# MLP up tiles as 512-column matmuls over high and low rows, with the rows' two parts stored next to each other

## The chip, the cores and the metric

The kernel runs on one core of one Trainium2 chip. The metric is the device time of one execution in microseconds. Before the change it is 1320.01 us, the median of 3 runs (1319.76 to 1320.15).

## The reference

One sequence of 256 tokens with 1024 features goes through two stacks in float32. The first stack: an RMS norm and an input projection; two recurrent mixers (a gated delta rule and HGRN2) on halves of the features; an output projection; the MLP; a gated embedding. The second stack: a convolution mixer with 16 meta tokens ahead of the sequence, then a product-key expert layer over 16384 experts, computed densely, and a final norm. The part that the change is about is the MLP of the first stack:

```python
u = jnp.einsum('btd,df->btf', rms_norm(h, pre_mlp_norm[i]), w_mlp_up[i])
y = jnp.einsum('btf,fd->btd', jnp.square(jax.nn.relu(u)), w_mlp_down[i])
h = h + rms_norm(y, post_mlp_norm[i])
```

with `w_mlp_up` of 1024 x 4096 and `w_mlp_down` of 4096 x 1024.

## The kernel before

**Weights.** All large weights are one stream of tiles of 128 x 1024 float32 values (512 KB), which SyncE loads into a ring of four slots. Each tile is split into two float32r parts: ScalarE copies the high part `w_hi` (`hi`, L1285 to L1292), and VectorE, or GpSimd in some stages, subtracts it from the tile to get the low part `w_lo` (`lo`, L1898 to L1904). There are two slots for the parts (`S = 2`), so the split of tile g+2 waits until TensorE has used tile g. The rows x, kept transposed in `hT_hi` and `hT_lo`, are split in the same way. A product is three matmuls: high by high, the weights' high by the rows' low, the weights' low by the rows' high.

**Rows.** `hT_hi` and `hT_lo` are two tensors of 8 blocks of 128 features; a block has META + T = 272 columns (16 meta tokens, 256 tokens), 1088 bytes in each partition. Six times in the kernel the normalised rows are transposed into them: for the input projection, the output projection, the MLP, the gate, the second input projection, and the query projection with the experts' first layer. `hT_at` (L344) tells where the 256 tokens begin: column 0 or, for the gate and the second input projection, column 16.

**Two kinds of tile.** `out_block` (L618) makes features by tokens: the stationary operand is a 128 x 128 block of the weights, the moving operand 256 columns of the rows. `passes` (L600) puts out the matmuls: for each of 8 blocks k the pair `w_hi` by high rows and `w_hi` by low rows, then the signal `hi_used`, a wait for `lo_done`, and 8 matmuls with `w_lo`; 24 in all, in one bank's first 256 columns. `row_tile` (L653) makes tokens by features: the stationary operand is 128 tokens of the rows, the moving operand 512 columns of the weights; 12 matmuls. `first_block` (L623) is the first tile after a transposition and mixes the three kinds of product, since its rows come block by block. Tiles of the first kind are the f, q and qkv projections (20 tiles), the MLP's up tiles (32), the second input projection (20), the query projection (16) and the experts' first layer (128). Tiles of the second kind are the i, z and g projections (12, through `rows_of`), the output projections, the MLP's down tiles (32), the embedding, the gate and the experts' second layer.

**The MLP.** It has four rounds of 8 up tiles and 8 down tiles. An up tile m writes bank 4 + m % 4. When it is done, ScalarE takes Relu of the bank into `relu` (L1479), and VectorE squares it into `mid` (L2187), casts that to `mid_hi` (L2190) and subtracts to get `mid_lo` (L2192). Each step waits for the one before by a semaphore (`relu_out`, `mid_step`, `mid_out`). The down tiles accumulate into banks 0 to 3, with `mid_hi` and `mid_lo` as stationary operands. The order on each engine is the order in which the code lists it: on ScalarE the split of a later tile's `w_hi` and then Relu, on VectorE the split of `w_lo` and then the three steps.

## Time and profile before

| | us |
|---|---|
| median of 3 runs | 1320.01 |
| the profiled execution | 1318.27 |
| its span, from the first to the last instruction | 1316.5 |
| TensorE busy with matmuls | 1291.7 |
| VectorE busy | 1007.4 |
| ScalarE busy | 789.9 |
| GpSimd busy | 444.6 |

The time of an execution is longer than its span by what lies around the first and the last instruction. Times are microseconds, from the span's start, unless marked ns. PE is TensorE's matmul side, DVE is VectorE, ACT is ScalarE. A tile's name stands for the tensor (`arena` is the big buffer that holds `relu`, `mid` and much else; `bank` is one of 8 PSUM banks). In the view of groups a line has the code line, the engine, the operation, output<-inputs, shapes, the count, and after the bar the busy time, the mean duration of one, and the idle time ahead of it with what ended it. The durations of matmuls are from the start to the modelled end, and neighbours overlap. In the timeline a line begins with the start and the duration; a number after x says how many instructions were merged.

### The profile page before, as it was taken

The page shows a single profiled execution, that of the slowest core. Times are in us where ns is not written, and L with a number is a line of the kernel's source. Part 1 is how long each engine was busy: PE and PEld are TensorE (multiplying, and loading weights), DVE is VectorE, ACT ScalarE, POOL GpSimd, SP SyncE. Part 2 cuts the span into 40 slices and gives each one's busy share as a digit, 9 for nine tenths or more (in the row PEclk, how much of TensorE's full clock was granted, in tenths as well). Part 3 has the DMA queues.
Part 4 walks back from the last instruction along what each step waited for, and adds up shares of the span by engine and source line. Part 5 has one row for each costly group of instructions (what it writes and reads, how often), then busy time and mean ns, then how long its engine had stood idle before and what let it go on. Part 6 is the DMA issues. An engine that isn't in the chain of part 4 may idle for free.

```text
span 1316.5 us, 24954 instructions
## 1 busy us (share of the span) xinstructions
PE 1291.7 (98%) x8852; PEld 1183.3 (90%) x8852; DVE 1007.4 (77%) x1890; ACT 789.9 (60%) x1414; POOL 444.6 (34%) x255
## 2 busy tenths in 40 slices
PE   7999999999999999999999999999999999999997
PEld 7998988989977997999999999999998888888886
DVE  4787658656666985689997777887636899999996
ACT  6545445444466455467776777777656566666664
POOL 2100415000023754038888777777750000000000
PEclk9999999999999999999999999999999999999999
DMA  8533126666654544555656555555567666555553
GB/s 304 177 113 113 33 96 203 191 191 191 184 169 134 170 132 130 171 161 177 190 179 188 161 161 161 160 161 160 158 195 224 222 197 206 199 201 192 195 190 112
DMA packets 64657, 225.49 MB, mean 171 GB/s; under 512 B 7200, under 2 KB 7712, under 8 KB 64176
## 3 DMA queue, kind: packets, MB, share of 16 engines
q1 hardware_dynamic: 62832, 218.36, 53.1%
q10 hardware_dynamic: 1728, 5.84, 1.2%
q8 instruction: 61, 1.00, 0.3%
q14 instruction: 36, 0.29, 0.1%
HBM read 223.12 MB, written 1.05 MB: 170 GB/s over the span
## 4 chain that ended last, share of the span: by engine, by line
PE 93%; DVE 4%; issue 1%; ACT 1%; DMA 0%; POOL 0%; SPq 0%; POOLq 0%; DVEq 0%; ACTq 0%
PE bank L613 76%; PE bank L1154 2%; PE bank L1185 2%; PE bank L1182 2%; PE bank L1181 2%; PE bank L714 1%; PE bank L862 1%; PE bank L848 1%; DVE w_lo L1903 1%; PE bank L1109 1%; PE bank L595 1%; PE bank L670 0%; DVE arena L2269 0%; PE bank L1017 0%; DMA cols<-in_cols 0%
## 5 line engine op out<-in xcount | busy, mean ns | idle before, releaser
L1292 ACT ACTIVATE w_hi<-ring 128x1024 fp32r<-128x1024 f32 x380 | 402.5, 1060 | 381.4 <-issue 197.5
L613 PE MATMUL bank<-hT_hi,w_hi 128*128 128x256 f32 (+2 forms) x1696 | 420.3, 286 | 0.0
L613 PE MATMUL bank<-hT_lo,w_hi 128*128 128x256 f32 (+2 forms) x1696 | 412.6, 282 | 0.0
L1903 DVE TENSOR_TENSOR w_lo<-ring,w_hi 128x1024 fp32r<-128x1024 f32 x225 | 275.3, 1224 | 143.1 <-ACT w_hi L1292 140.1
L1855 POOL TENSOR_TENSOR w_lo<-ring,w_hi 128x1024 fp32r<-128x1024 f32 x128 | 310.9, 2431 | 143.0 <-ACT w_hi L1292 142.8
L613 PEld LDWEIGHTS bank<-hT_lo,w_hi 128*128 128x128 f32 x1696 | 320.0, 189 | 0.4
L613 PEld LDWEIGHTS bank<-hT_hi,w_hi 128*128 128x128 f32 x1696 | 318.9, 188 | 0.4
L613 PE MATMUL bank<-hT_hi,w_lo 128*128 128x256 f32 (+2 forms) x1696 | 234.8, 280 | 0.0
L613 PEld LDWEIGHTS bank<-hT_hi,w_lo 128*128 128x128 f32 x1696 | 215.9, 189 | 0.0
L1752 POOL TENSOR_SCALAR mstat<-mstat 128x1 f32<-128x1 f32 x16 | 6.1, 383 | 537.7 <-ACT bank L1249 334.4
L613 PE MATMUL bank<-w_hi,wgt_hi 128*128 128x512 f32 x368 | 143.4, 390 | 0.2 <-DVE wgt_lo L2515 0.2
L613 PE MATMUL bank<-w_hi,wgt_lo 128*128 128x512 f32 x368 | 143.2, 389 | 0.0
L613 PE MATMUL bank<-w_lo,wgt_hi 128*128 128x512 f32 x368 | 98.4, 389 | 0.0
L1646 ACT ACTIVATE wgt_hi<-arena 128x256 fp32r<-128x256 f32 x116 | 47.0, 406 | 63.6 <-PE bank L613 60.5
L613 PEld LDWEIGHTS bank<-w_hi,wgt_hi 128*128 128x128 f32 x368 | 69.1, 188 | 15.3 <-issue 1.1
L613 PEld LDWEIGHTS bank<-w_lo,wgt_hi 128*128 128x128 f32 x368 | 69.1, 188 | 14.4
L613 PEld LDWEIGHTS bank<-w_hi,wgt_lo 128*128 128x128 f32 x368 | 69.1, 188 | 14.2
L1634 ACT ACTIVATE consts<-consts,idxT 128x128 f16<-128x128 f16 x256 | 81.1, 392 | 0.0
L1816 POOL TENSOR_TENSOR w_lo<-ring,w_hi 128x1024 fp32r<-128x1024 f32 x26 | 62.8, 2414 | 25.9 <-ACT w_hi L1292 24.5
L2515 DVE TENSOR_TENSOR wgt_lo<-arena,wgt_hi 128x256 fp32r<-128x256 f32 x128 | 55.3, 432 | 5.4 <-ACT wgt_hi L1646 5.4
L2502 DVE TENSOR_TENSOR arena<-arena,bank 128x256 f32<-128x256 f32 (+35 forms) x80 | 24.4, 305 | 41.9 <-ACT bank L1620 19.0
L2480 DVE TENSOR_TENSOR consts<-bank,idxT 128x512 f16<-128x512 f32 x64 | 44.2, 691 | 12.1 <-ACT consts L1634 9.8
(395 smaller groups left out, 2077.8 us busy)
## 6 DMA issues: line engine op xcount, KB each, us to landing
ring<-in_stream SPq DMA_DIRECT2D x380, 512.0 KB, 3.6
arena<-in_stream SPq DMA_DIRECT2D x34, 512.0 KB, 4.6
arena<-in_rows ACTq DMA_DIRECT2D x1, 1536.0 KB, 10.8
consts<-in_consts ACTq DMA_DIRECT2D x1, 1152.0 KB, 6.0
arena<-in_keys ACTq DMA_DIRECT2D x1, 1024.0 KB, 5.0
h<-in_x SPq DMA_DIRECT2D x2, 256.0 KB, 3.9
h<-in_x ACTq DMA_DIRECT2D x2, 256.0 KB, 3.9
arena<-in_rows ACTq DMA_DIRECT2D x1, 512.0 KB, 4.6
```

Of the source, the lines that this page charges most:

```text
L613: mm = nc.tensor.matmul(o, a, b, start=first and not low_part and xp is x[0], stop=last and low_part)
L1154: mm = nc.tensor.matmul(bank[half][:, n * P:(n + 1) * P], hot2[:, half, n, :], hotg[:, half, i, n, :], start=i == 0, stop=i == 1)
L1181: nc.tensor.matmul(bank[b][:, :], x[0], w, start=first and b >= 4, stop=False)
L1182: nc.tensor.matmul(bank[b][:, :], x[1], w, start=False, stop=False)
L1292: nc.scalar.activation(w_hi[:, g % S, :], ring[:, g % R, :], ACT.Copy).then_inc(hi_done, 1)
L1634: ins = nc.scalar.activation(hotg[:, s % 2, 0, n, :], hot1[:, n, :], ACT.Copy, scale=idxT[:, 2, 4 * s + n:4 * s + n + 1])
L1646: nc.scalar.activation(wgt_hi[:, j % 2, :], act_all[:, at, :], ACT.Copy).then_inc(wgt_step, 1)
L1816: nc.gpsimd.tensor_tensor(w_lo[:, g % S, :], ring[:, g % R, :], w_hi[:, g % S, :].bitcast(F32), ALU.subtract).then_inc(lo_done, 1)
L1855: nc.gpsimd.tensor_tensor(w_lo[:, g % S, :], ring[:, g % R, :], w_hi[:, g % S, :].bitcast(F32), ALU.subtract).then_inc(lo_done, 1)
L1903: nc.vector.tensor_tensor(w_lo[:, g % S, :], ring[:, g % R, :], w_hi[:, g % S, :].bitcast(F32), ALU.subtract).then_inc(lo_done, 1)
L2480: nc.vector.tensor_tensor(hot1, over(iota_bank, 4), spread(idxT[:, 0, tok], P), ALU.is_equal)\
L2515: nc.vector.tensor_tensor(wgt_lo[:, j % 2, :], at, wgt_hi[:, j % 2, :].bitcast(F32), ALU.subtract)\
```

## The change

It does four things.

1. The two tensors become one, `hT`, and a second view of the same bytes is added: `x_both`, with 8 blocks of 2048 bytes in each partition, 256 high columns and then 256 low ones. The four stages without meta tokens use this view (`x_hi`, `x_lo`, `x_cut`); the gate and the second input projection keep the old one.
2. An up tile of the MLP (`up_block`) issues for each block k one matmul of 512 columns, `w_hi` by high and low rows together, and then the 8 matmuls of `w_lo` by the high rows as before. High products and low products of the rows thus stand in the two halves of a bank. The first up tile writes its low products to the second half too, with the old 24 matmuls.
3. The sum of the halves and the activation: ScalarE copies the low half to `up`, VectorE adds the other half from the bank, and then makes max(u, 0) * u in one instruction.
4. The cast to `mid_hi` moves from VectorE to ScalarE, and it and the subtraction for `mid_lo` come one tile later in their engines' order, behind the split of the next weights.

```diff
@@ -147,8 +147,10 @@
         ring = sb("ring", [P, R, D])
         w_hi = sb("w_hi", [P, S, D], F32R)
         w_lo = sb("w_lo", [P, S, D], F32R)
-        hT_hi = sb("hT_hi", [P, KD, META + T], F32R)
-        hT_lo = sb("hT_lo", [P, KD, META + T], F32R)
+        hT = sb("hT", [P, 2, KD, META + T], F32R)
+        hT_hi, hT_lo = hT[:, 0, :, :], hT[:, 1, :, :]
+        x_both = hT.rearrange("p a k n -> p (a k n)")[:, 0:2 * KD * T].rearrange("p (k a t) -> p k a t", k=KD, a=2)
+        x_hi, x_lo = x_both[:, :, 0, :], x_both[:, :, 1, :]
         h = sb("h", [P, NT, D])
         consts = sb("consts", [P, NCONST])
         cols = sb("cols", [P, NCOLS])
...
@@ -341,7 +343,8 @@
                 eng.wait_ge(tiles_done, rows_end[stage])
 
         block_cols = ["pre_mix", None, "pre_mlp", None, "mix2", "ffn2"]
-        hT_at = [0, 0, 0, META, META, 0]
+        rows_in_view = [(x_hi, x_lo) if n not in (3, 4) else (hT_hi[:, :, META:META + T], hT_lo[:, :, META:META + T])
+                        for n in range(6)]
 
         def block_scale(n, k):
 
...
@@ -492,6 +495,8 @@
         yT_high, yT_ready = sem("yT_high"), sem("yT_ready")
         keys_loaded, scores_full = sem("keys_loaded"), sem("scores_full")
 
+        up_low, up_low0 = vt_out, 1
+        mid_high, mid_high0 = kt_out, 1
         pair_loaded, pair_loaded0 = meta_in_sb, 16
         pair_sums, pair_sums0 = dbias, 2
         pair_hi, pair_hi0 = decays, 2
...
@@ -615,14 +623,29 @@
                 mm.then_inc(tiles_done, 1)
                 return mm
 
-            def out_block(w, o, cols_of):
-
-                passes(w, [(o, hT_cut(k, cols_of), slice(k * P, (k + 1) * P), True, k == 0, k == KD - 1)
+            def out_block(w, o, rows_of=x_cut):
+
+                passes(w, [(o, rows_of(k), slice(k * P, (k + 1) * P), True, k == 0, k == KD - 1)
                            for k in range(KD)])
 
-            def first_block(w, o, cols_of, n, lag=0):
+            def up_block(w, b):
 
                 slot, low = w
+                both = bank[b][:, :]
+                for k in range(KD):
+                    mm = nc.tensor.matmul(both, w_hi[:, slot, k * P:(k + 1) * P], x_both[:, k, :, :],
+                                          start=k == 0, stop=False)
+                mm.then_inc(hi_used, 1)
+                pe.wait_ge(lo_done, low)
+                for k in range(KD):
+                    mm = nc.tensor.matmul(bank[b][:, 0:T], w_lo[:, slot, k * P:(k + 1) * P], x_hi[:, k, :],
+                                          start=False, stop=k == KD - 1)
+                mm.then_inc(tiles_done, 1)
+
+            def first_block(w, o, n, lag=0, rows_of=x_cut, apart=None):
+
+                slot, low = w
+                o_low = o if apart is None else apart
 
                 def part(k):
                     return slice(k * P, (k + 1) * P)
...
@@ -631,20 +654,20 @@
 
                     if k == 0:
                         pe.wait_ge(lo_done, low)
-                    return nc.tensor.matmul(o, w_lo[:, slot, part(k)], hT_hi[:, k, cols_of], start=False, stop=k == KD - 1)
+                    return nc.tensor.matmul(o, w_lo[:, slot, part(k)], rows_of(k)[0], start=False, stop=k == KD - 1)
 
                 if tr_bank[n]:
                     pe.wait_ge(tr_lo, KD * n + 2)
                 for k in range(KD):
                     pe.wait_ge(tr_hi, KD * n + k + 1)
-                    nc.tensor.matmul(o, w_hi[:, slot, part(k)], hT_hi[:, k, cols_of], start=k == 0, stop=False)
+                    nc.tensor.matmul(o, w_hi[:, slot, part(k)], rows_of(k)[0], start=k == 0, stop=False)
                     if lag <= k < KD - 1 + lag:
                         low_product(k - lag)
                     if k:
                         pe.wait_ge(tr_lo, KD * n + k)
-                        nc.tensor.matmul(o, w_hi[:, slot, part(k - 1)], hT_lo[:, k - 1, cols_of], start=False, stop=False)
+                        nc.tensor.matmul(o_low, w_hi[:, slot, part(k - 1)], rows_of(k - 1)[1], start=False, stop=False)
                 pe.wait_ge(tr_lo, KD * n + KD)
-                nc.tensor.matmul(o, w_hi[:, slot, part(KD - 1)], hT_lo[:, KD - 1, cols_of], start=False, stop=False)\
+                nc.tensor.matmul(o_low, w_hi[:, slot, part(KD - 1)], rows_of(KD - 1)[1], start=False, stop=False)\
                     .then_inc(hi_used, 1)
                 for k in range(KD - max(lag, 1), KD):
                     mm = low_product(k)
...
@@ -925,7 +948,7 @@
                     mm.then_inc(oa_full, 1)
 
             def out_lhs(j, t):
-                return hT_cut(OUT_ORDER[j], slice(t * P, (t + 1) * P))
+                return x_cut(OUT_ORDER[j], slice(t * P, (t + 1) * P))
 
             pe.wait_ge(gdn_gated, 4)
             for j in range(6):
...
@@ -955,8 +978,8 @@
                 s = (G_MLP + m) % S
                 pe.wait_ge(hi_done, i * 16 + (G_MLP + m + 1))
 
-                pe.wait_ge(relu_out, i * 8 + m + 1)
-                out_block((s, i * 16 + (G_MLP + m + 1)), bank[4 + m % 4][:, 0:T], slice(0, T))
+                pe.wait_ge(up_out, i * 8 + m + 1)
+                up_block((s, i * 16 + (G_MLP + m + 1)), 4 + m % 4)
 
             def mlp_round(i, closing):
 
...
@@ -1279,7 +1302,7 @@
                     if k % 2 == 0:
                         act.wait_ge(tr_full, 4 * n + k // 2 + 1)
                     src = bank[tr_bank[n] + k // 2][:, (k % 2) * T:(k % 2 + 1) * T]
-                    nc.scalar.activation(hT_hi[:, k, hT_at[n]:hT_at[n] + T], src, ACT.Copy, scale=block_scale(n, k))\
+                    nc.scalar.activation(rows_in_view[n][0][:, k, :], src, ACT.Copy, scale=block_scale(n, k))\
                         .then_inc(tr_hi, 1)
 
             def hi(g, round_=0, per=0):
...
@@ -1471,14 +1493,21 @@
 
             def mlp_round(i, closing):
 
+                def mid_copy(m):
+
+                    act.wait_ge(mid_step, i * 8 + m + 1)
+                    nc.scalar.activation(mid_hi[:, m, :], mid[:, m % 2, :], ACT.Copy).then_inc(mid_high, 1)
+
                 for m in range(8):
                     hi(G_MLP + m + S, i, 16)
+                    if m:
+                        mid_copy(m - 1)
                     act.wait_ge(tiles_done, i * 16 + (G_MLP + m + 1))
-
-                    act.wait_ge(mid_out, i * 8 + m + 1)
-                    nc.scalar.activation(relu[:, m % 2, :], bank[4 + m % 4][:, 0:T], ACT.Relu).then_inc(relu_out, 1)
+                    nc.scalar.activation(up[:, m % 2, :], bank[4 + m % 4][:, T:2 * T], ACT.Copy).then_inc(up_low, 1)
                 for m in range(8, 14 if closing else 16):
                     hi(G_MLP + m + S, i, 16)
+                    if m == 8:
+                        mid_copy(7)
                     if closing and m < 12:
                         h_squares(2, 0, m - 8)
 
...
@@ -2177,22 +2206,31 @@
             dve.wait_ge(lo_done, G_MLP + 1)
             los(G_OUT + 7, 1)
             dve.sem_inc(mid_out, 2)
+            dve.sem_inc(up_out, 4)
+
+            def mid_low(i, m):
+
+                dve.wait_ge(mid_high, i * 8 + (mid_high0 + m + 1))
+                nc.vector.tensor_tensor(mid_lo[:, m, :], mid[:, m % 2, :], mid_hi[:, m, :].bitcast(F32),
+                                        ALU.subtract).then_inc(mid_out, 1)
 
             def mlp_round(i, closing):
 
                 for m in range(8):
                     lo(G_MLP + m + S, i, 16)
-
-                    dve.wait_ge(relu_out, i * 8 + m + 5)
-                    nc.vector.tensor_tensor(mid[:, m % 2, :], relu[:, m % 2, :], relu[:, m % 2, :], ALU.mult)\
-                        .then_inc(mid_step, 1)
-                    dve.wait_ge(mid_step, i * 16 + 2 * m + 1)
-                    nc.vector.tensor_copy(mid_hi[:, m, :], mid[:, m % 2, :]).then_inc(mid_step, 1)
-                    dve.wait_ge(mid_step, i * 16 + 2 * m + 2)
-                    nc.vector.tensor_tensor(mid_lo[:, m, :], mid[:, m % 2, :], mid_hi[:, m, :].bitcast(F32),
-                                            ALU.subtract).then_inc(mid_out, 1)
+                    if m:
+                        mid_low(i, m - 1)
+
+                    dve.wait_ge(up_low, i * 8 + (up_low0 + m + 1))
+                    nc.vector.tensor_tensor(up[:, m % 2, :], up[:, m % 2, :], bank[4 + m % 4][:, 0:T], ALU.add)\
+                        .then_inc(up_out, 1)
+                    dve.wait_ge(up_out, i * 8 + m + 5)
+                    nc.vector.scalar_tensor_tensor(mid[:, m % 2, :], up[:, m % 2, :], 0.0, up[:, m % 2, :],
+                                                   ALU.max, ALU.mult).then_inc(mid_step, 1)
                 for m in range(8, 14 if closing else 16):
                     lo(G_MLP + m + S, i, 16)
+                    if m == 8:
+                        mid_low(i, 7)
 
             with dve.Fori(0, MLP_ROUNDS - 1) as i:
                 mlp_round(i, False)
```

The query projection and the experts' tiles change in the same way as the projections, `hT_cut(k, slice(0, T))` to `x_cut(k)`.

## Rows read from the trace of the kernel before

**Rows 1.** The page's busy times, and the chain that ended last by engine.

```profile
PE 1291.7 (98%) x8852; PEld 1183.3 (90%) x8852; DVE 1007.4 (77%) x1890; ACT 789.9 (60%) x1414; POOL 444.6 (34%) x255
...
PE 93%; DVE 4%; issue 1%; ACT 1%; DMA 0%; POOL 0%; SPq 0%; POOLq 0%; DVEq 0%; ACTq 0%
```

**Rows 2.** Windows, MLP: length, busy of PE, PEld, DVE, ACT, POOL, clock, DMA.

```profile
201.00:380.00 179.00, 178.86 (x1154) 162.86 (x1152) 116.47 (x171) 83.78 (x115) 21.26 (x31) 1.00 0.63 190
```

**Rows 3.** Groups by form, whole span: a 256-column product, two 256-wide operations.

```profile
L613 PE MATMUL bank<-hT_hi,w_hi 128*128 128x256 f32 x1576 | 389.1, 285 | 0.0
...
L1646 ACT ACTIVATE wgt_hi<-arena 128x256 fp32r<-128x256 f32 x116 | 47.0, 406 | 63.6 <-PE bank L613 60.5 <-PE bank L1185 3.1
...
L2269 DVE SCALAR_TENSOR_TENSOR arena<-bank,cols,arena 128x256 f32<-128x256 f32 x104 | 43.0, 476 | 2.9 <-ACT arena L1533 2.5
```

**Rows 4.** Timeline of TensorE, up tiles: starts of three, one's w_lo products.

```profile
254.77 0.28 PE L613 MATMUL bank<-hT_hi,w_hi 128*128 128x256 f32 x1
...
256.67 1.11 PE L613 MATMUL bank<-hT_hi,w_lo 128*128 128x256 f32 x8
257.61 0.28 PE L613 MATMUL bank<-hT_hi,w_hi 128*128 128x256 f32 x1
...
260.45 0.28 PE L613 MATMUL bank<-hT_hi,w_hi 128*128 128x256 f32 x1
```

**Rows 5.** Timeline of TensorE, down tiles: the first matmul of two neighbours.

```profile
235.37 0.39 PE L613 MATMUL bank<-w_hi,mid_hi 128*128 128x512 f32 x1
...
238.09 0.39 PE L613 MATMUL bank<-w_hi,mid_hi 128*128 128x512 f32 x1
```

**Rows 6.** Timeline of TensorE, output projection: first matmuls for k = 7, 0, 1.

```profile
182.55 0.40 PE L613 MATMUL bank<-w_hi,hT_hi 128*128 128x512 f32 x1
...
185.35 0.39 PE L613 MATMUL bank<-w_hi,hT_hi 128*128 128x512 f32 x1
...
188.09 0.40 PE L613 MATMUL bank<-w_hi,hT_hi 128*128 128x512 f32 x1
```

**Rows 7.** Chain in order of time (start, us, what): two tiles of the projections.

```profile
109.43 2.84 PE bank L613 x12
...
114.21 2.79 PE bank L613 x12
```

**Rows 8.** Timeline of TensorE, products with wab_both: blocks 0, 1, 4, 5; what follows.

```profile
53.34 0.28 PE L736 MATMUL bank<-hT_hi,wab_both 128*16 128x256 f32 x1
...
53.57 0.28 PE L736 MATMUL bank<-hT_hi,wab_both 128*16 128x256 f32 x1
...
54.27 0.28 PE L736 MATMUL bank<-hT_hi,wab_both 128*16 128x256 f32 x1
...
54.50 0.28 PE L736 MATMUL bank<-hT_hi,wab_both 128*16 128x256 f32 x1
...
55.19 0.28 PE L613 MATMUL bank<-hT_hi,w_hi 128*128 128x256 f32 x1
```

**Rows 9.** Timeline of VectorE, one up tile and the next split.

```profile
249.53 1.23 DVE L1903 TENSOR_TENSOR w_lo<-ring,w_hi 128x1024 fp32r<-128x1024 f32 x1 [1.67 <-ACT w_hi L1292]
250.67 0.42 DVE L2187 TENSOR_TENSOR arena<-arena 128x256 f32<-128x256 f32 x1
251.12 0.29 DVE L2190 CAST mid_hi<-arena 128x256 fp32r<-128x256 f32 x1
251.45 0.43 DVE L2192 TENSOR_TENSOR mid_lo<-arena,mid_hi 128x256 fp32r<-128x256 f32 x1
252.37 1.23 DVE L1903 TENSOR_TENSOR w_lo<-ring,w_hi 128x1024 fp32r<-128x1024 f32 x1 [0.49 <-ACT w_hi L1292]
```

**Rows 10.** Timeline of ScalarE, one up tile.

```profile
256.87 1.06 ACT L1292 ACTIVATE w_hi<-ring 128x1024 fp32r<-128x1024 f32 x1 [1.43 <-PE bank L613]
257.89 0.38 ACT L1479 ACTIVATE arena<-bank 128x256 f32<-128x256 f32 x1
```

**Rows 11.** Windows, columns as before: a stretch of the query projection.

```profile
521.00:524.00 3.00, 3.00 (x15) 3.00 (x15) 3.00 (x7) 1.12 (x4) 0.00 (x0) 0.50 0.53 175
```

45 lines of the change are left out of this document (23 added, 22 removed).

## The prediction

> **What bounds the kernel now.** I read the page's busy times first, and then the chain that ended last: TensorE is busy for 98% of the span and holds 93% of the chain [rows 1]. Next comes the stretch of the MLP, 201 to 380 us: TensorE is busy for 178.86 of the 179.00 us at the full clock, VectorE for 116 and ScalarE for 84 [rows 2]. So in the MLP a nanosecond counts only if TensorE saves it, and the other engines matter only once they make it wait. The view of groups says how one matmul looks, but its mean (285 ns) is from start to end of instructions that overlap [rows 3]. What a matmul costs is the distance between starts, so I go to the timeline. An up tile is 24 matmuls of 256 columns; three tiles start at 254.77, 257.61 and 260.45, so a tile takes 2.84 us and a matmul 118.3 ns [rows 4]. A down tile is 12 matmuls of 512 columns and takes 2.72 us, 226.7 ns each [rows 5]. Both send 6144 columns, which at 2.4 GHz is 2.56 us. What is above that is a surcharge per matmul: 0.28 us over 24 is 11.7 ns, 0.16 us over 12 is 13.3 ns. It hardly depends on the width, so fewer and wider matmuls are cheaper.
>
> **The change, part by part.**
>
> *The up tiles on TensorE.* In a tile, 16 matmuls of 256 columns (w_hi against high and low rows) become 8 of 512; the 8 of w_lo stay at 256. The before trace has no 512-column matmul with x as the moving operand, but the down tiles have the same form, with a stationary 128x128 block and 512 moving columns that begin on a multiple of 2048 bytes. I take their price: 8 x 226.7 + 8 x 118.3 = 2760 ns against 2840, so 80 ns a tile [rows 4, 5]. 31 of the 32 up tiles take the new form; the first one (`first_block`) keeps its 24 matmuls and only puts the low products in the other half of the bank. 31 x 0.080 = **2.5 us less**, all of it on the path, since the engine is never idle there [rows 2]. Bounds: 0, if two 256-column matmuls with one block cost no more than one of 512; and 31 x 8 x 13.3 ns = 3.3 us, if every removed matmul takes the larger surcharge with it.
>
> A sentence by itself: the Trainium skill, page "TensorE: Matmul & The Clock Gate", section "Back-to-back issue gap", puts the warm gap at N/2.4 + 2.5 ns; by it two matmuls of 256 columns cost 218.3 ns and one of 512 215.8, which would make this term 31 x 8 x 2.5 ns = 0.6 us. The trace does not agree: its two widths carry 11.7 and 13.3 ns [rows 4, 5].
>
> *The layout as stationary operand.* In the i, z and g projections (12 tiles) and the output projection (8 tiles) the rows are the stationary operand. Before, a block k begins at 1088 x k bytes, afterwards every piece begins on a multiple of 512. The timeline has both cases: the output tile that starts at 182.55 (k = 7, off a multiple of 256) takes 2.80 us, the next one (k = 0, on it) 2.74 [rows 6], and the down tiles, always on one, 2.72 [rows 5]. The pieces of the chain in the projections take 2.79 to 2.84 us for their 12 matmuls [rows 7]. I take 0.07 x 12 = 0.84 us there and 0.08 for the 6 output tiles other than k = 0 and 4, 0.48 us: **1.3 us less**. Bounds: 0 (it isn't the address), and 20 tiles x 0.10 = 2.0 us. The gate tiles keep the old view with its 16 columns ahead, and change nothing.
>
> *The layout as moving operand.* This is the uncertain part, because it reaches far beyond the MLP. The group of 256 columns has 1576 of each of its three kinds of product, 197 tiles [rows 3]. Without the 4 tiles that stay in the old view, and counting what is left of the up tiles and three first tiles, that is 162 x 24 + 31 x 8 + 3 x 24 = 4208 matmuls whose moving rows now begin on a multiple of 1024 bytes. In no tile before do all the moving blocks lie on such addresses. The nearest row is that of the 16 small products with `wab_both`: from 53.34 to 55.19, 115.6 ns each, with moving rows on every residue of the old layout and a stationary block of only 16 columns [rows 8]. Lower bound: 115.6, so 4208 x -2.7 = -11.4 us. Upper bound: the surcharge of the 512-column matmuls, whose operands are all aligned, 106.7 + 13.3 = 120.0 ns, so 4208 x 1.67 = +7.0 us. I take **0**: the up tiles keep 2.84 us exactly although their eight blocks lie on eight different residues [rows 4], which speaks for a rate that the address doesn't set. Both ends go into the range.
>
> *VectorE in an up tile.* Before: w_lo split, square, cast, subtraction; starts at 249.53, 250.67, 251.12, 251.45, end at 251.88, and the next split at 252.37 after 0.49 us of idle time [rows 9]. After: w_lo split (1.14 to the next start), `mid_low` of the tile before (0.45), the addition that reads the bank (0.48 at most, as the operation that reads a bank in [rows 3], plus 0.05 for its semaphore), max-times (0.43): 2.55 us in a period of 2.76. Cost 0; TensorE hides it. 0.2 us of slack is left of 0.49.
>
> *ScalarE.* Before: w_hi split 1.06 and Relu 0.38 [rows 10]. After: 1.06 + the copy to `mid_hi` (0.41, [rows 3]) + the copy of the low half (0.38) = 1.85 us of 2.76. There is a new wait: `mid_copy(m-1)` waits for VectorE's max-times of m-1. Queued behind it on ScalarE are the copy of tile m, for which VectorE's addition waits, and the w_hi split of tile m+3. In time after the end of tile m: ScalarE's split ends at about +0.3 (it starts 0.2 after the w_lo products begin [rows 4, 10]), the copies end at +0.7 and +1.1. VectorE is through its split at +1.5 and `mid_low` at +1.9, adds until +2.4 and has the product at +2.85. The copy that needs it wants to start at 2.76 + 0.3 = +3.06. It fits with 0.2 us. TensorE needs w_hi of m+2 at +2.76, has it at +0.3; and the bank of tile m four tiles later. Cost 0. If the cover went, the loop ScalarE-VectorE would set the tile time, and 0.1 us too much is 31 x 0.1 = 3.1 us.
>
> *The rest.* The first down tile of a round wants `mid_low(0)`, which was made six tiles earlier; `mid_low(7)` is made during the first down tiles and used by the eighth. SP's ring loads keep their order and gates; a tile period of 2.76 us asks for less than the 2.72 of the down tiles gets now. The pair products address the same bytes as before. All 0, and could not gain.
>
> **Sum.** -2.5 - 1.3 + 0 = -3.8 us. The profiled execution took 1318.27 us (span 1316.5 and 1.8 around it): 1314.5. It lies 1.74 below the median of the runs, 1320.01, so for the median: **1316.2 us**.
>
> **The rivals.**
> *A, aligned 256-column matmuls are slower.* The end on the other side. Mechanism: if the surcharge belongs to the addresses as in the all-aligned down tiles, each of the 4208 costs up to 120.0 ns. For: 13.3 is more than 11.7 [rows 4, 5]. Against: the wider matmul also moves twice the data, and among the `wab_both` products the block at residue 0 is no slower than that at residue 256 (0.23 us for either pair) [rows 8]. Price up to +7.0: 1323.2. It cancels the gain from 0.9 ns per matmul (119.2) and makes the kernel slower by over 0.2% from 1.5 ns.
> *B, they are faster.* For: alignment helps the stationary operand by 6 ns [rows 6], so it may help the moving one. Against: the constant 2.84. Half of the lower bound, 117.0 ns, gives -5.7: 1310.5; all of it 1304.8.
> *C, the ScalarE-VectorE loop becomes the bound* in the up tiles, with a new wait in place of covered work. For: slack falls from 0.49 to 0.2. Against: the sum above. At 0.1 us a tile: 1319.3.
> *D, the change doesn't do what it says:* 8 x 512 take as long as 16 x 256, since the block's load was hidden anyway. Only the stationary part remains: 1318.7. Against: [rows 4, 5].
> *E, the clock.* Three stretches ran at half clock, 1.2 GHz, one of them at 521 to 524 us, in the first tile of the query projection [rows 11]; 15 of its matmuls took 3.00 us instead of 1.78, some 1.4 us over the whole stretch. All work behind the MLP comes 3 us earlier, so one such stretch may go or come: 1314.8 or 1317.6.
>
> **How the numbers follow.** Forecast 0.50 (its own range 1314.2 to 1318.2, 0.4 ns per aligned matmul and E's small shifts), A 0.18, B 0.18, C 0.05, D 0.05, E alone 0.04. 0.2% is 2.6 us, about what can be told from no change: faster means below 1317.4. Faster: 0.36 of the forecast's 0.50, 0.17 of B, 0.01 of E = 0.54. Same: 0.14 + 0.08 of A + 0.01 of B + 0.03 of C + 0.05 of D + 0.02 of E = 0.33. Slower: 0.10 of A + 0.02 of C + 0.01 of E = 0.13. The range leaves out the far half of B (0.09) and the far end of A (0.04) and little else: 1310.0 to 1322.5.
>
> **What would show it.** Up tiles that start 2.76 us apart, 226.7 ns between 512-column matmuls and 118.3 between the w_lo ones; output tiles at 2.72; tiles of the query projection and of the expert stage still at 2.84 (2.86 and above is A, 2.81 and below B, and there the whole forecast stands or falls); idle time of some 0.2 us before VectorE's split, and none on TensorE between 204 and 372 us. It is wrong if the expert tiles change, if the up tiles stay at 2.84, or if TensorE waits in them for the bank or for `w_hi`.

## The result, and the profile after the change

The changed kernel takes 1321.99 us (median of 12 runs, 1320.26 to 1324.15) against 1319.84 for the kernel before in the same runs (12 runs, 1316.92 to 1321.62): ratio 1.0021, interval 1.0013 to 1.0029. It is slower by 0.2%, where 1316.2 was forecast. The profiled execution took 1320.26 us, its span 1318.4.

The page's busy times and the chain by engine, which answer to [rows 1]:

```profile
PE 1292.8 (98%) x8604; PEld 1174.5 (89%) x8604; DVE 1006.1 (76%) x1890; ACT 798.3 (61%) x1446; POOL 443.9 (34%) x255
...
PE 93%; DVE 4%; issue 1%; ACT 1%; POOL 0%; ACTq 0%; POOLq 0%; DVEq 0%
```

248 matmuls are gone (8852 to 8604), and yet TensorE is busy for 1.1 us more. Nothing else moved on the chain. So the loss is in how long matmuls take, and I add up stages. Each goes from its first start on TensorE to the first start of what follows; the MLP and the experts' second layer go to the start of their last matmul.

| stage | before | after | difference | forecast |
|---|---|---|---|---|
| input projections up to the i tiles (with wab) | 64.94 | 65.64 | +0.70 | 0 |
| i, z, g tiles and what follows them | 93.24 | 92.85 | -0.39 | -0.84 |
| output projection | 27.13 | 26.77 | -0.36 | -0.48 |
| MLP | 178.05 | 176.51 | -1.54 | -2.5 |
| query projection and the experts' first layer | 451.87 | 455.81 | +3.94 | 0 |
| experts' second layer | 337.72 | 337.45 | -0.27 | 0 |

The differences add up to +2.1 us, as the two executions and the medians differ (+2.0, +2.15).

The timeline of TensorE in the changed kernel's MLP, columns as in [rows 4] (start, duration, instruction, how many merged):

```profile
254.14 2.00 PE L636 MATMUL bank<-hT,w_hi 128*128 128x512 f32 x8
255.98 1.12 PE L641 MATMUL bank<-hT,w_lo 128*128 128x256 f32 x8
256.94 2.00 PE L636 MATMUL bank<-hT,w_hi 128*128 128x512 f32 x8
258.78 1.11 PE L641 MATMUL bank<-hT,w_lo 128*128 128x256 f32 x8
```

An up tile takes 256.94 - 254.14 = 2.80 us (2.793 on average) where [rows 4] had 2.84 and 2.76 was forecast. The eight wide matmuls last 1.84 us to the start of the `w_lo` products, 230 ns each instead of 226.7.

The windows that answer to [rows 2] and [rows 11], columns as there:

```profile
201.00:378.00 177.00, 176.85 (x906) 151.05 (x904) 116.99 (x170) 91.47 (x147) 20.56 (x31) 1.00 0.63 192
```

```profile
521.00:524.00 3.00, 2.99 (x24) 2.80 (x24) 2.51 (x4) 1.33 (x2) 0.00 (x0) 1.00 0.29 117
```

TensorE waits no more than before, 0.15 us in 177. The stretch at half clock of [rows 11] is not there: the granted clock is 1.00 in it. That gave something back, so the loss in the experts is larger than 3.94; against `wide_only` below (451.00 us, full clock there too) it is 4.81.

Where it comes from shows in two w_lo groups of neighbouring expert tiles, first of the kernel before, then of the changed one:

```profile
641.77 1.11 PE L613 MATMUL bank<-hT_hi,w_lo 128*128 128x256 f32 x8
...
644.61 1.11 PE L613 MATMUL bank<-hT_hi,w_lo 128*128 128x256 f32 x8
```

```profile
640.66 1.12 PE L621 MATMUL bank<-hT,w_lo 128*128 128x256 f32 x8
...
643.54 1.12 PE L621 MATMUL bank<-hT,w_lo 128*128 128x256 f32 x8
```

2.84 us apart, then 2.88: 118.3 ns a matmul before and 120.0 after, with the same instructions in the same order. In the view of groups 2656 high and 1328 low products of this form are left outside the up tiles:

```profile
L621 PE MATMUL bank<-hT,w_hi 128*128 128x256 f32 x2656 | 351.6, 285 | 0.0
L621 PE MATMUL bank<-hT,w_lo 128*128 128x256 f32 x1328 | 186.1, 283 | 0.0
```

The high products' mean is the 285 ns of [rows 3], so the loss is easily overlooked in this view. It measures overlapping instructions from start to end, and its means also mix stages: inside the experts' loop alone the mean goes from 281 to 283 ns.

The output projection, which answers to [rows 6]:

```profile
182.70 1.98 PE L621 MATMUL bank<-w_hi,hT 128*128 128x512 f32 x8
...
185.42 1.98 PE L621 MATMUL bank<-w_hi,hT 128*128 128x512 f32 x8
...
188.14 1.07 PE L621 MATMUL bank<-w_hi,hT 128*128 128x512 f32 x4
```

Both tiles take 2.72 us, as forecast for rows as the stationary operand on multiples of 512.

VectorE and ScalarE in an up tile, which answer to [rows 9] and [rows 10]:

```profile
257.28 1.23 DVE L1932 TENSOR_TENSOR w_lo<-ring,w_hi 128x1024 fp32r<-128x1024 f32 x1 [0.44 <-ACT w_hi L1315]
258.42 0.42 DVE L2214 TENSOR_TENSOR mid_lo<-arena,mid_hi 128x256 fp32r<-128x256 f32 x1
258.76 0.41 DVE L2225 TENSOR_TENSOR arena<-arena,bank 128x256 f32<-128x256 f32 x1
259.20 0.42 DVE L2228 SCALAR_TENSOR_TENSOR arena<-arena 128x256 f32<-128x256 f32 x1
260.07 1.23 DVE L1932 TENSOR_TENSOR w_lo<-ring,w_hi 128x1024 fp32r<-128x1024 f32 x1 [0.44 <-ACT w_hi L1315]
```

```profile
256.18 1.06 ACT L1315 ACTIVATE w_hi<-ring 128x1024 fp32r<-128x1024 f32 x1 [1.16 <-PE bank L636]
257.15 0.40 ACT L1499 ACTIVATE mid_hi<-arena 128x256 fp32r<-128x256 f32 x1
257.45 0.37 ACT L1506 ACTIVATE arena<-bank 128x256 f32<-128x256 f32 x1
```

VectorE still has 0.44 us of idle time in a period of 2.79 (0.2 was forecast), and ScalarE 1.16. Their new work costs nothing.

### The profile page after: what moved, and what is told of

Same layout as the page of the kernel before. It is cut to its first block, busy times and chain, and to the rows that moved or that the text cites. A ratio compares the mean times of both kernels' runs of the same rounds, so it can differ in the third digit from the quotient of the medians.

```text
span 1318.4 us, 24443 instructions
## 1 busy us (share of the span) xinstructions
PE 1292.8 (98%) x8604; PEld 1174.5 (89%) x8604; DVE 1006.1 (76%) x1890; ACT 798.3 (61%) x1446; POOL 443.9 (34%) x255
## 4 chain that ended last, share of the span: by engine, by line
PE 93%; DVE 4%; issue 1%; ACT 1%; POOL 0%; ACTq 0%; POOLq 0%; DVEq 0%
PE bank L621 69%; PE bank L636 4%; PE bank L1177 2%; PE bank L641 2%; PE bank L1204 2%; PE bank L1205 2%; PE bank L1208 2%; PE bank L737 1%; PE bank L885 1%; DVE w_lo L1932 1%; PE bank L871 1%; PE bank L1132 1%; PE bank L693 0%; DVE arena L2307 0%; PE bank L1040 0%
## 5 line engine op out<-in xcount | busy, mean ns | idle before, releaser
L621 PE MATMUL bank<-hT,w_hi 128*128 128x256 f32 (+1 forms) x2896 | 384.7, 285 | 0.0
L621 PEld LDWEIGHTS bank<-hT,w_hi 128*128 128x128 f32 x2896 | 360.1, 191 | 0.6
L621 PE MATMUL bank<-hT,w_lo 128*128 128x256 f32 (+1 forms) x1448 | 203.2, 283 | 0.0
L621 PEld LDWEIGHTS bank<-hT,w_lo 128*128 128x128 f32 x1448 | 187.0, 192 | 0.0
L636 PE MATMUL bank<-hT,w_hi 128*128 128x512 f32 x248 | 62.0, 392 | 0.0
L636 PEld LDWEIGHTS bank<-hT,w_hi 128*128 128x128 f32 x248 | 44.8, 189 | 8.1
```

The source lines that it names most:

```text
L621: mm = nc.tensor.matmul(o, a, b, start=first and not low_part and xp is x[0], stop=last and low_part)
L636: mm = nc.tensor.matmul(both, w_hi[:, slot, k * P:(k + 1) * P], x_both[:, k, :, :], start=k == 0, stop=False)
```

## The experiments

The question is what makes the unchanged 256-column matmuls slower, and what the wide ones are worth without it. In the experiments the places of the rows are a table, `X_AT`: for stage 0 (input projections), 1 (output projection), 2 (MLP) and 5 (query projection and experts) the column where the high rows begin, the column where the low ones begin, and the distance between blocks, in columns of 4 bytes. A stage that is not in it keeps the old places. The code fixes distances, not addresses: `w_hi`, `w_lo` and `hT` stand one behind the other, `w_hi` and `w_lo` take 8192 bytes each, and weight blocks are 512 bytes apart, so offset 0 is a multiple of 512 bytes away from every weight block. Where the first tensor begins is up to the build, and no run here varies it. So "on a multiple of 512" in the texts below, and "residue", are to be read as a distance from the weights. Of each edit only the table is shown; the code that reads it is left out, and lines that begin with `+#` are explanations. Columns of the fences are those of [rows 4].

### One part alone: layout_only and wide_only

`layout_only` is the kernel before with the new places and the 24 narrow matmuls:

```diff
+X_AT = {0: (0, 256, 512), 1: (0, 256, 512), 2: (0, 256, 512), 5: (0, 256, 512)}
```

> The kernel before with nothing changed but the place of the rows: blocks of 2048 bytes, high next to low, in the four stages without meta tokens. Up tiles keep their 24 matmuls of 256 columns. Address theory (a 256-column matmul whose operands all begin on multiples of 512 bytes carries the surcharge of the down tiles, 13.3 ns, 120.0 in all): up tiles and expert tiles 2.88 us instead of 2.84, 195 tiles and three first ones, so 198 x 0.04 = +7.9 us, less 1.3 us for the rows as stationary operand: +6.6 us, 1326.4. Rival, the new ScalarE-VectorE chain or the 512-column matmuls cost the time: expert tiles stay at 2.84, and the kernel is 1.3 us faster than before.

`wide_only` is the changed kernel with the new places in the MLP alone:

```diff
-        x_both = hT.rearrange("p a k n -> p (a k n)")[:, 0:2 * KD * T].rearrange("p (k a t) -> p k a t", k=KD, a=2)
...
+        X_AT = {2: (0, 256, 512)}
```

> The changed kernel with the new places for the rows in the MLP alone; the input, output and query projections and the experts have the old blocks of 1088 bytes. Address theory: the expert tiles are back at 2.84 us, the MLP keeps the 1.5 us that it gained in the changed kernel (up tiles 2.79), so 1.5 us faster than before, 1318.3. Rival, the expert stage is slower for another reason (its first tile, the clock, the order in front of it): it stays at 455.8 us from the first query tile to the first second-layer tile, and the kernel is slower than before by some 2 us.

Both against 1318.88 us for the kernel before: `layout_only` 1324.94 (ratio 1.0042, 1.0027 to 1.0056), `wide_only` 1316.51 (0.9979, 0.9970 to 0.9989). Expert tiles of `layout_only`, then of `wide_only`:

```profile
640.07 1.12 PE L632 MATMUL bank<-hT,w_lo 128*128 128x256 f32 x8
...
642.95 1.12 PE L632 MATMUL bank<-hT,w_lo 128*128 128x256 f32 x8
```

```profile
641.57 1.10 PE L637 MATMUL bank<-hT,w_lo 128*128 128x256 f32 x8
...
644.41 1.10 PE L637 MATMUL bank<-hT,w_lo 128*128 128x256 f32 x8
```

2.88 us with the new places and 2.84 without them; the query projection and the experts take 455.82 us in `layout_only`, as in the changed kernel (455.81). So the places make the loss there, all of it, and the MLP goes from 178.05 to 176.46 us in `wide_only`. Of its 2.4 us, 0.87 are in the query projection and the experts (451.00 for 451.87), where the half-clock stretch at 521 us is missing too.

The places cost something in the MLP as well: with narrow matmuls at the new places (`layout_only`) it takes 179.21 us, with wide ones at the same places 176.51. At equal places the wide form saves 2.70 us, 87 ns a tile, and 40 ns of these only make good what the places cost. The two halves of the change pull against each other, and the layout, which serves the MLP's 31 tiles, is charged to 144 others and to the 20 of the first projections.

### Which property of the places: residues_a and residues_b

Three things changed at once: the residue of the start, the high rows' block lying next to the low one, and that all blocks have the same residue. Each stage tries another combination.

```diff
+# residues_a: 64 bytes later; blocks of 2112 bytes in the MLP; high and low apart, on multiples of 512, in the experts
+X_AT = {0: (16, 272, 512), 1: (0, 256, 512), 2: (0, 256, 528), 5: (0, 2176, 256)}
+# residues_b: high and low apart; output 2112; MLP blocks of 2176 bytes; experts 64 bytes later
+X_AT = {0: (0, 2176, 256), 1: (0, 256, 528), 2: (0, 256, 544), 5: (16, 272, 512)}
```

> The kernel before, with another place of the rows in each stage, to read the time of a 256-column matmul in the trace. First projections: blocks of 2048 bytes, all 64 bytes past a multiple of 512. MLP: blocks of 2112 bytes, so that the eight blocks lie on eight residues of 512 as before, with high next to low. Query and experts: high blocks of 1024 bytes on multiples of 512, the low ones 8704 bytes on. Three theories. T1, a block on a multiple of 512 is slow in itself: 118 or less in the projections, 118.3 in the MLP, 120.0 in the experts. T2, high next to low is slow: 120.0, 120.0, 118.3. T3, an equal place of all blocks is slow and changing residues are fast: 120.0, 118.3, 120.0.

> As the run before, with the places exchanged. First projections: high blocks of 1024 bytes on multiples of 512, low ones 8704 bytes on. Output projection: blocks of 2112 bytes. MLP: blocks of 2176 bytes, residues 0, 128, 256, 384. Query and experts: blocks of 2048 bytes, all 64 bytes past a multiple of 512. T1 (multiples of 512 are slow): 120.0, MLP between 118.3 and 120.0, experts 118 or less. T2 (neighbours are slow): 118.3, 120.0, 120.0. T3 (equal places are slow): 120.0, 118.3, 120.0.

Times of one run each: 1322.59 and 1315.12. The input projections of `residues_a` (64 bytes later), then those of `residues_b` (apart, on multiples of 512):

```profile
34.37 1.07 PE L632 MATMUL bank<-hT,w_lo 128*128 128x256 f32 x8
...
37.09 1.07 PE L632 MATMUL bank<-hT,w_lo 128*128 128x256 f32 x8
```

```profile
34.59 1.12 PE L632 MATMUL bank<-hT,w_lo 128*128 128x256 f32 x8
...
37.47 1.12 PE L632 MATMUL bank<-hT,w_lo 128*128 128x256 f32 x8
```

2.72 against 2.88 us. Blocks of the same size and neighbourhood as in the changed kernel, only 64 bytes later, cost 113.3 ns a matmul and not 120.0 in the first seven tiles, and 117.8 in some of the later ones. High and low far apart changes nothing. In the MLP, blocks that run over all residues (2112 bytes) give 2.84 as in [rows 4], and blocks on 0 and 128 modulo 256 give 2.81. So it is the residue (T1), and neither the neighbourhood nor the equal places.

A tile is not the mean of its residues, though. T1 had 2.84 to 2.88 for the mix of 0 and 128, and 2.81 is less than a tile with all blocks on 0 (2.88) or all on 128 (2.85, below). What the trace of the kernel before shows is that the starts within an up tile are 115 to 122 ns apart, in the same pattern in every tile. The 2.84 that looked constant was a sum over unequal distances; how a matmul's neighbours enter into them stays open.

### Which residues: uniform_a, uniform_b, wide_a, wide_b

```diff
+# uniform_a, narrow: 128 bytes in the projections, 256 in the MLP, 192 in the experts
+X_AT = {0: (32, 288, 512), 1: (0, 256, 512), 2: (64, 320, 512), 5: (48, 304, 512)}
+# uniform_b, narrow: 32, 128 (output), 384 (MLP), 448 (experts)
+X_AT = {0: (8, 264, 512), 1: (32, 288, 512), 2: (96, 352, 512), 5: (112, 368, 512)}
+# wide_a, 512-column up tiles: 16, 256 (output), 64 (MLP), blocks of 2176 bytes (experts)
+X_AT = {0: (4, 260, 512), 1: (64, 320, 512), 2: (16, 272, 512), 5: (0, 256, 544)}
+# wide_b, 512-column up tiles: 320, 0, blocks of 2112 bytes (MLP), 256 (experts)
+X_AT = {0: (80, 336, 512), 1: (0, 256, 512), 2: (0, 256, 528), 5: (64, 320, 512)}
```

> The kernel before with blocks of 2048 bytes, high next to low, all eight at one distance past a multiple of 512: 128 bytes in the first projections, 256 in the MLP, 192 in the query projection and the experts; the output projection on multiples of 512. What is known: at distance 0 a 256-column matmul takes 120.0 ns, at 64 it took 117.8 in the experts and either 113.3 or 117.8 in the projections. Theory X (only a start on a multiple of 512 is slow): 118 or less at 128, 256 and 192, so tiles of 2.83 us or less. Rival Y (what counts is whether the start is a multiple of 256, as for the rows as stationary operand): 120.0 at 256, so MLP up tiles of 2.88; 118 or less at 128 and 192. Rival Z (a multiple of 128 is slow): 120.0 at 128 and 256.

> As the run before, with distances of 32 bytes in the first projections, 384 in the MLP, 448 in the query projection and the experts, and 128 in the output projection. X: 118 ns or less everywhere. Y: the same. Z: 120.0 at 384, 118 or less at 32 and 448. The output projection (rows as stationary operand, 512 columns) is expected at 2.79 to 2.80 us a tile, since 128 is not a multiple of 256. If the rate has two states at one distance, as at 64 bytes, tiles of 2.72 and of 2.83 us stand side by side in one stage.

> The changed kernel (512-column matmuls in the up tiles) with other distances past a multiple of 512: 16 bytes in the first projections, 256 in the output projection, 64 in the MLP, and blocks of 2176 bytes (distances 0, 128, 256, 384) for the query projection and the experts. If the 27 ns by which the eight 512-column matmuls of an up tile exceed 8 x 226.7 come from starts on a multiple of 512, the up tile falls from 2.79 to 2.74 us or less; if they come from the change of width after the 256-column matmuls, it stays at 2.79 (w_lo products at 117.8 would take 17 ns off). Experts: 117.2 ns as the MLP had with this place, 2.81 us a tile, so 3 us less than before in the stage. Output projection at 2.72 us a tile (256 is as good as 0).

> The changed kernel with distances of 320 bytes in the first projections, 0 in the output projection, blocks of 2112 bytes in the MLP (eight distances) and 256 bytes for the query projection and the experts. X: 118 ns or less at 256, experts 2.83 us. Y and Z: 120.0, 2.88. The up tile with eight distances: 2.79 us or more, if unequal places hinder the 512-column matmul as they do the 256-column one (118.3 against 117.8), 2.74 if they don't.

One run each, beside 1318.34 for the kernel before: 1309.59, 1310.18, 1314.26, 1320.90. First the MLP of `uniform_a` at 256 bytes, then its query projection at 192:

```profile
252.34 1.12 PE L632 MATMUL bank<-hT,w_lo 128*128 128x256 f32 x8
...
255.22 1.12 PE L632 MATMUL bank<-hT,w_lo 128*128 128x256 f32 x8
```

```profile
570.14 1.07 PE L632 MATMUL bank<-hT,w_lo 128*128 128x256 f32 x8
571.05 1.98 PE L632 MATMUL bank<-hT,w_hi 128*128 128x256 f32 x16
572.87 1.07 PE L632 MATMUL bank<-hT,w_lo 128*128 128x256 f32 x8
```

2.88 and 2.73. A start 256 bytes later is as slow as 0, so X (only multiples of 512 are slow) is refuted and Y fits there. At 128 and 384 Y's "118 or less" is missed by a little, and most tiles at 384 take Z's 120.0. The output projection of `uniform_b` takes 2.79, as expected. Over all runs the narrow tiles, 24 matmuls each, are these:

| start of the moving rows, bytes | us a tile | ns a matmul |
|---|---|---|
| 0 or 256 | 2.880 | 120.0 |
| 128 | 2.847 | 118.6 |
| 384 | 2.845 to 2.852 for seven tiles, then 2.880 | 118.5 to 120.0 |
| 16 | 2.847, 2.80 and, for two tiles, 2.72 | 118.6, 116.7, 113.3 |
| 32 | 2.80 | 116.7 |
| 64, 192, 320, 448 | 2.827 or 2.720 | 117.8 or 113.3 |
| over all residues (before) | 2.840 | 118.3 |
| 0 and 128 by turns | 2.813 | 117.2 |

The odd multiples of 64 have two rates, and groups of 8 short matmuls between tiles switch between them. In the query projection of `uniform_a` the rate changes at every such group, from 2.720 to 2.828 and back; the experts' loop, which has none, runs at 2.827 throughout, and from the point where the gate groups (8 short matmuls behind a tile) begin, tiles take 2.720, or 2.813 to 2.818 with the step after the group in it. Stage 5 took 441.10 us at 192 and 440.32 at 448, against 451.87 before; before and at 192 it holds a stretch of 3.4 us at half clock, at 448 none.

The four odd multiples are not alike there. In all runs with 192 or 448 the gate stretch is fast. With 64 (`residues_b`, 449.54 us) it stays at 2.827, and the query projection too.

In the up tiles the wide form reacts in another way. The MLP of `wide_a`, 64 bytes later:

```profile
251.89 2.00 PE L652 MATMUL bank<-hT,w_hi 128*128 128x512 f32 x8
253.72 1.07 PE L657 MATMUL bank<-hT,w_lo 128*128 128x256 f32 x8
254.63 1.99 PE L652 MATMUL bank<-hT,w_hi 128*128 128x512 f32 x8
256.46 1.11 PE L657 MATMUL bank<-hT,w_lo 128*128 128x256 f32 x8
```

Here tiles mostly alternate between 2.741 and 2.772 us, on average the 2.76 of the forecast: the eight wide matmuls last 1.83, where they last 1.84 in the changed kernel, and the narrow ones 0.91 or 0.94 instead of 0.95. At residues of 2112-byte blocks (`wide_b`) an up tile takes 2.80. So for the wide ones 64 bytes make next to nothing, and the aligned place costs the tile through its `w_lo` products. Neither reading of the up tiles in the expectation came out: of the 27 ns above 8 x 226.7, 16 remained. Its output tiles (2.72) and its expert tiles (2.81) did.

### The changed kernel 64 bytes later: shift_64

```diff
-        x_both = hT.rearrange("p a k n -> p (a k n)")[:, 0:2 * KD * T].rearrange("p (k a t) -> p k a t", k=KD, a=2)
+        x_both = hT.rearrange("p a k n -> p (a k n)")[:, 16:16 + 2 * KD * T].rearrange("p (k a t) -> p k a t", k=KD, a=2)
```

> The changed kernel with one number changed: the view of the rows begins 64 bytes later, so that no block begins on a multiple of 256. If the place of the moving rows is what made the changed kernel slower than before, the expert tiles fall from 2.88 us to 2.83 in the first 48 and to 2.72 or 2.81 after the first gate group, as they did in the runs at distances 192 and 448: the stage takes 441 us instead of 455.8. The first projections take 63.8 instead of 65.6, the MLP 175.7 instead of 176.5, and the projections with the rows as stationary operand lose 0.9: some 16 us less than the changed kernel, 1306. Rival (distance 64 is worse than 192 and 448 in the experts, as its steady 2.83 in the loop showed before the gate groups; the other two had the same there): 453 us for the stage, 1318.

1314.63 us against 1318.84, ratio 0.9961 (0.9946 to 0.9975). One number in the changed kernel turns it from 0.2% slower to 0.4% faster. The expectation was too good by 8 us, because I had counted on the rate of 113.3 in the experts. The expert tiles stayed at 2.83 instead:

```profile
639.97 1.10 PE L621 MATMUL bank<-hT,w_lo 128*128 128x256 f32 x8
640.91 2.05 PE L621 MATMUL bank<-hT,w_hi 128*128 128x256 f32 x16
642.79 1.10 PE L621 MATMUL bank<-hT,w_lo 128*128 128x256 f32 x8
```

Behind the loop, after six short matmuls, two tiles fell to 2.72 (from 705.57 to 708.29; in `residues_b` they didn't), and the first gate group threw them back to 2.827, with 2.913 to 2.918 for the tiles behind a gate group (`uniform_a`: 2.813 to 2.818). The stage took 449.22, near the 449.54 of `residues_b`, also at 64: the rival, that 64 is worse than 192 and 448 in the experts, is what came, if not in its full size (453). As the stationary operand, 64 bytes cost: the output projection takes 27.30 us, 0.5 more than in the changed kernel. The i, z and g stage takes 94.37, but it begins with a stretch at reduced clock that lasted longer here (granted 0.67 from 76 to 86 us, 0.83 in the changed kernel); against `layout_only`, which had 0.70 there and 94.12 us, 0.25 more is left.

### The best of each: best and best_kick

```diff
+# 64 bytes for projections and MLP, 0 for the output projection, 192 for query and experts
+X_AT = {0: (16, 272, 512), 1: (0, 256, 512), 2: (16, 272, 512), 5: (48, 304, 512)}
```

> The changed kernel with a place of the rows for each stage: 64 bytes past a multiple of 512 in the first projections and the MLP, on multiples of 512 in the output projection (stationary operand), 192 bytes past in the query projection and the experts. By the sums of the stages measured one by one: first projections -1.2 us against the kernel before, output projection -0.4, MLP -2.4, query and experts -10.8: 15 us less, 1304.

`best_kick` adds eight matmuls with zeros behind expert tile 1 (counted from 0), to push the loop from one rate to the other. For that, the first four expert tiles are written out ahead of the loop:

```diff
+            for e in range(PEER_BODY):
+                w = tile(G_PEER + e)
+                pe.wait_ge(gel_out, e + 1)
+                out_block(w, bank[4 + e][:, 0:T])
+                if e == 1:
+                    pe.wait_ge(sc_out, NHH // 2)
+                    for n in range(8):
+                        nc.tensor.matmul(bank[0][:, 0:P], zb, zb, start=True, stop=True)
```

> The run before with 8 small matmuls of zeros (bf16, 128 columns) after the second expert tile, into a bank that is free then, and the first four expert tiles written out instead of looped. The 256-column matmuls at odd multiples of 64 bytes have run at 113.3 or at 117.8 ns in one and the same stage, and changed from the slower to the faster state at the first gate group. If the group's small matmuls are what changed it, the 44 tiles of the loop now take 2.72 us instead of 2.83: 0.107 x 44 = 4.7 us less than the run before, less 0.5 us for the small matmuls: 1300. If it was something else (the end of the loop, the transposes of the routing), no change or 0.5 us more.

`best`: 1304.21 us against 1318.84, ratio 0.9884 (0.9868 to 0.9901). `best_kick`: 1302.61, ratio 0.9880 (0.9863 to 0.9896). The experts' loop in `best`, then in `best_kick`, from its tile 1 on:

```profile
640.87 1.11 PE L637 MATMUL bank<-hT,w_lo 128*128 128x256 f32 x8
641.81 2.05 PE L637 MATMUL bank<-hT,w_hi 128*128 128x256 f32 x16
643.70 1.11 PE L637 MATMUL bank<-hT,w_lo 128*128 128x256 f32 x8
```

```profile
575.52 1.10 PE L637 MATMUL bank<-hT,w_lo 128*128 128x256 f32 x8
576.47 0.62 PE L1173 MATMUL bank<-zeros 128*128 128x128 bf16 x8
576.90 2.07 PE L637 MATMUL bank<-hT,w_hi 128*128 128x256 f32 x16
578.80 1.07 PE L637 MATMUL bank<-hT,w_lo 128*128 128x256 f32 x8
...
641.93 1.07 PE L637 MATMUL bank<-hT,w_lo 128*128 128x256 f32 x8
...
644.65 1.07 PE L637 MATMUL bank<-hT,w_lo 128*128 128x256 f32 x8
```

2.827 against 2.720: the same instructions at the same places, and eight short matmuls some tiles ahead decide which. The rate changes at the zeros: the two written-out tiles ahead of them still run at the slow rate, the next one starts its matmuls 113 ns apart. So writing the tiles out is not what does it.

Stage 5 falls from 441.10 to 437.41 us, but 0.8 of these 3.7 us is the clock: the first query tile takes 5.01 us in `best` (granted clock 0.66) and 4.23 in `best_kick` (1.00). The rest, 2.9 us, is what the other rate is worth, where 4.2 were expected: three tiles took 3.0 us, TensorE waiting 0.2 us in each for GpSimd's split of `w_lo`, and the last of the loop 3.08. The medians differ by 1.6 us where their intervals overlap, so that the second is faster than the first as a whole isn't shown; that its loop runs at the other rate is.

### Address or distance: weights_off

The weights stayed where they were until here, so the residue of the rows could be one of their address or of their distance from the weights. This kernel moves `w_hi` and `w_lo` by 64 bytes, with the narrow up tiles.

```diff
+        sb("ahead_of_weights", [P, 16])
         w_hi = sb("w_hi", [P, S, D], F32R)
         w_lo = sb("w_lo", [P, S, D], F32R)
+        sb("behind_weights", [P, 112])
+X_AT = {0: (16, 272, 512), 1: (0, 256, 512), 2: (0, 256, 512), 5: (48, 304, 512)}
```

> The kernel before (24 matmuls of 256 columns in the up tiles) with all weight parts w_hi and w_lo moved 64 bytes past a multiple of 512, and rows at 64 in the first projections, at 0 in the output projection and the MLP, at 192 in the query projection and the experts. If what counts is the distance between moving and stationary address (R), the rates move with it: 120.0 ns in the first projections (difference 0), and the MLP's up tiles fast, 2.83 us or less (difference 64). If each address counts by itself (S), the MLP stays at 120.0 or gets slower still, since its stationary operand now starts off a multiple of 256 (+6 ns for the 512-column matmuls), and the down tiles, whose moving operand now starts at 64, tell what that does to 512 columns: 2.72 us if nothing.

1321.35 us (one run). Its input projections, rows and weights both 64 bytes off, and its MLP, rows at 0 and weights at 64:

```profile
34.94 1.12 PE L634 MATMUL bank<-hT,w_lo 128*128 128x256 f32 x8
35.90 2.08 PE L634 MATMUL bank<-hT,w_hi 128*128 128x256 f32 x16
37.82 1.12 PE L634 MATMUL bank<-hT,w_lo 128*128 128x256 f32 x8
```

```profile
250.41 1.07 PE L634 MATMUL bank<-hT,w_lo 128*128 128x256 f32 x8
251.32 1.98 PE L634 MATMUL bank<-hT,w_hi 128*128 128x256 f32 x16
253.13 1.07 PE L634 MATMUL bank<-hT,w_lo 128*128 128x256 f32 x8
```

2.88 and 2.72. The places that were fast in `residues_a` (rows at 64) are slow when the weights are at 64 too, and rows at 0, slow everywhere else, are fast. In the experts (rows 192, weights 64) tiles take 2.847, as at 128 above. What counts is the distance between the starts of the moving and the stationary operand, modulo 256 as far as it was tried. The down tiles, whose distance became 64, went from 2.72 to 2.747, which fits the other sign for 512 columns. The output projection says the same (weights at 64, rows at 0: 2.747), and the other direction costs more (rows at 64, weights at 0, in `shift_64`: 2.80). The i, z and g stage, with both at 64, takes 92.92 us, about the 92.85 of the changed kernel with both at 0, where rows alone at 64 (`residues_a`) gave 93.39: there too it is the distance.

Its MLP, in the old form of 24 narrow matmuls, takes 175.07 us: less than the changed kernel's 176.51 and than `wide_a`'s 175.68, although its down tiles are slower. Its up tiles take 2.72, the changed ones 2.79. In this stage, with the operands 64 bytes apart, the wide matmul isn't needed. The kernel as a whole is not faster, since its other stages got the worse distances: the first projections are back at 2.88, and the experts' second layer, 512 columns of weights at 64, takes 341.05 us for 337.72.

## Why the prediction was wrong

**The failed step: the layout as moving operand, "I take 0".** In its place the runs show 120.0 ns for 118.3 in uninterrupted tiles, +5.5 us in the stages outside the MLP. It was rival A at its upper end, 120.0 ns. That A had it to the digit is luck in part: it took 13.3 ns from the down tiles as the surcharge of aligned addresses, and with 512 columns the aligned place is the cheapest (226.7 ns; 228.9 and 233.3 were measured off it). The forecast price was up to +7.0 us for 4208 matmuls; the stages show +0.70 and +4.81 at equal clock, 5.5 in all. It is less than 7.0 since tiles that are interrupted by other matmuls mostly lose 24 to 29 ns and not 40 (a tile with a gate group 3353 ns before and 3380 after), and since the share of the MLP's `w_lo` products stands in the MLP's row. Two arguments misled me. "The up tiles keep 2.84 although their blocks lie on eight residues" [rows 4] was read as a rate that the address doesn't set; a tile is a sum over all eight, its starts are 115 to 122 ns apart, and the sum is constant all the same. And the pairs with `wab_both` [rows 8] compared residue 0 with 256, which are one case (2.88 us at either), so their being equal said nothing. They were no stand-in for the tiles either: the blocks of `wab_both` are 64 bytes apart, and these 16 products got faster with the new places, 1.81 us for 1.85.

**Rival A's time**, 1323.2 at full price, is near what came, 1321.99.

**The up tiles, -2.5.** Fewer and wider matmuls are cheaper, as forecast, but the size was off: -1.54 measured (-1.59 in `wide_only`), 47 ns a tile for 80. (Against narrow matmuls at the same places it is -2.70, but the forecast compared with the old places.) Of the missing 33 ns, 27 are in the wide matmuls: in the trace they start 227 ns apart at the end of a group, but 228 to 236 in its first five, behind the narrow ones. The other 6 are the `w_lo` products, six of which are at 120. The price came from down tiles, where no such change is.

**Rows as stationary operand, -1.3.** Right in the output projection (-0.36 for -0.48, tiles at 2.72); half of it in i, z and g (-0.39 for -0.84): there every tile comes after an interruption, and the first nine or so start mostly 228 to 236 ns apart and not 226.7. Both kernels had the same clock there (0.83 from 76 to 86 us).

**VectorE and ScalarE, 0; rival C.** Right. VectorE has 0.44 us left, more than the 0.2 forecast, since the addition starts 0.34 us after `mid_lo` and not 0.45, and the period is longer. No wait took its place.

**Rival D** (wide is no cheaper) is refuted by `wide_only`. **Rival E** happened: the half-clock stretch is gone, and gave back 451.87 - 451.00 = 0.87 us if `wide_only` is the comparison, a part of what hid the loss. **Rival B** (aligned is faster) is refuted for these tiles, and its price (115.6 ns at best) was no lower bound: 113.3 occurs.

The Trainium skill, page "TensorE: Matmul & The Clock Gate", section "Back-to-back issue gap", gives N/2.4 + 2.5 ns as the warm gap of an isolated matmul, which makes, as an estimate, 109.2 for 256 columns and 215.8 for 512. The gate groups, 128 columns of 16-bit values, do start 56 ns apart as it says. The fp32r matmuls of the tiles never come down to it: the lowest rates are 113.3 and 226.7. The formula has no term for a layout, and the traces show one.

**Open.** What in the chip makes the distance count, and the two rates at odd multiples of 64, is not shown. Nor is it shown why at 64 bytes the experts stay at the slow rate behind the gate groups (`shift_64`, `residues_b`) and at 192 and 448 they don't (`uniform_a`, `uniform_b`, `best`, `best_kick`).

## What to carry to other kernels

Before a layout is changed for one stage's sake, count all matmuls that read it: here 31 tiles gained 1.5 us and 144 others lost 4.8. In a TensorE-bound kernel the distance of the two operands' starts modulo 256 bytes is a tuning knob of its own (for 256 fp32r columns try odd multiples of 64, 192 first; for rows as a stationary operand under 512 columns 0). `best` gains 1.2% with it and the wide matmuls together, and 10.8 of its 14.6 us are in the query projection and the experts, where the places alone changed; `wide_only` gained 0.2%. A rate read from tiles that mix cases is the rate of that mix alone: look for a tile in which all parts lie as they will after the change, and give the step a chance of its own where there is none.

## What the runs showed of the hardware

- Back-to-back 256-column fp32r matmuls start 120.0 ns apart when moving and stationary operands begin at the same residue modulo 256, 118.6 or 120.0 at a distance of 128, and 117.8 or 113.3 at odd multiples of 64. A mix of distances 0 and 128 gives 117.2, less than either alone.
- The two rates at odd multiples of 64 can last for tens of tiles, and eight short matmuls throw the engine from one to the other: to the fast one in `best_kick`, to the slow one in `shift_64`, and to each by turns in the query projection of `best`.
- With 512 moving columns the equal residue is the cheap one: 226.7 ns, against 228.9 with the moving operand 64 bytes on (2.747 us for 12, `weights_off`) and 233.3 with the stationary one 64 bytes on (2.80 us, `shift_64`).
- After an interruption or a change of width the first wide matmuls start up to 236 ns apart, and 226.7 comes back after some five to nine.
- Stretches at half clock come and go at nearly the same places from kernel to kernel (521 to 524 us: 0.50 before, 1.00 after), which shifts a stage by about 1 us. Stage times compare only where the clock is the same.
